# Attention core of a hybrid backbone step: one guard and one transposed copy for both heads, transposes ahead of the values of an older item

## What is computed

```python
def attend_block(qb, keys, values, masks, sink):
    scale = HEAD_DIM ** -0.5
    ...
        s = jnp.einsum('bqkgd,bskd->bkgqs', qb, kp).astype(jnp.float32) * scale
        if mk is not None:
            s = jnp.where(mk, s, NEG_INF)
    ...
    m = sink_f
    for s in scores:
        m = jnp.maximum(m, jnp.max(s, axis=-1))
    denom = jnp.exp(sink_f - m)
    ...
        p = jnp.exp(s - m[..., None])
        denom = denom + jnp.sum(p, axis=-1)
        out = out + jnp.einsum('bkgqs,bskd->bqkgd', p.astype(vp.dtype), vp)
    out = out / jnp.moveaxis(denom, -1, 1)[..., None]
```

## Time and profile before

| | us |
|---|---|
| median of three runs | 2660.65 (2658.5 to 2661.7) |
| profiled execution | 2665.53 |
| its span in the trace | 2663.7 |
| TensorE busy | 2573.9 (97%) |
| TensorE weight loads busy | 2383.5 (89%) |
| VectorE busy | 1984.8 (75%) |
| ScalarE busy | 1299.1 (49%) |
| GpSimd busy | 115.5 (4%) |
| attention core of layer 0 | about 142.8 to 283.9 of the span |
| attention core of layer 3 | about 2013.6 to 2131.6 of the span |

### The profile page before, as it was taken

The page is one execution under the profiler, slowest core; times in us unless marked ns, Lnnn a source line. Parts: engine busy times, 40 slices in busy tenths (PEclk is TensorE's granted clock), DMA queues, the critical chain, the costliest instruction groups (busy, mean ns, idle before and its releaser), DMA issues.

```text
span 2663.7 us, 43103 instructions
## 1 busy us (share of the span) xinstructions
PE 2573.9 (97%) x15856; PEld 2383.5 (89%) x15856; DVE 1984.8 (75%) x3736; ACT 1299.1 (49%) x2291; POOL 115.5 (4%) x146
## 2 busy tenths in 40 slices
PE   6989999999998999999989999999998999999999
PEld 4966899999998999999879999999997699999998
DVE  3777488888896888888855888888868946754772
ACT  3467365425524663355244662454347936633551
POOL 2000100000012000000101000000100010000000
PEclk9999899999998999999989999999999999999999
DMA  7224122433341334434302335334320012222222
GB/s 292 64 95 148 58 101 104 163 138 118 108 168 48 103 110 160 154 105 146 124 21 72 116 111 184 111 110 153 118 71 29 2 56 72 78 87 64 76 83 78
DMA packets 72274, 279.64 MB, mean 105 GB/s; under 512 B 7888, under 2 KB 11344, under 8 KB 68560
## 3 DMA queue, kind: packets, MB, share of 16 engines
q1 hardware_dynamic: 72144, 277.93, 30.5%
HBM read 274.75 MB, written 3.15 MB: 104 GB/s over the span
## 4 chain that ended last, share of the span: by engine, by line
PE 89%; DVE 7%; issue 2%; ACT 1%; DMA 1%; POOL 0%; SPq 0%; DVEq 0%; ACTq 0%
PE ps L575 20%; PE ps L573 16%; PE ps L574 16%; PE ps L576 15%; PE ps L577 11%; PE ps L792 2%; PE ps L777 2%; PE ps L761 1%; PE ps L634 1%; DVE h L1406 1%; PE ps L687 1%; DVE prob L1609 1%; DVE ada_w L1352 1%; PE ps L828 1%; PE ps L569 1%
## 5 line engine op out<-in xcount | busy, mean ns | idle before, releaser
L575 PE MATMUL ps<-h,w_hi 128*128 128x512 f32 x1768 | 700.5, 396 | 0.0
L573 PE MATMUL ps<-h,w_hi 128*128 128x386 f32 x1768 | 604.8, 342 | 8.2 <-DVE h L1406 4.9
L574 PE MATMUL ps<-h,w_hi 128*128 128x386 f32 x1768 | 602.9, 341 | 0.0
L576 PE MATMUL ps<-h,w_lo 128*128 128x386 f32 x1768 | 598.7, 339 | 0.0
L950 ACT ACTIVATE tail<-ps 128x256 f32<-128x256 f32 x281 | 108.3, 386 | 966.0 <-PE ps L577 965.4
L577 PE MATMUL ps<-h,w_lo 128*128 128x256 f32 x1768 | 503.4, 285 | 0.0
L577 PEld LDWEIGHTS ps<-h,w_lo 128*128 128x128 f32 x1768 | 333.7, 189 | 79.6
L1293 DVE TENSOR_TENSOR w_lo<-w_raw,w_hi 128x1024 fp32r<-128x1024 f32 (+1 forms) x288 | 377.4, 1311 | 4.9 <-ACT w_hi L945 1.7
L573 PEld LDWEIGHTS ps<-h,w_hi 128*128 128x128 f32 x1768 | 339.3, 192 | 11.3 <-DVE h L1406 7.2
L574 PEld LDWEIGHTS ps<-h,w_hi 128*128 128x128 f32 x1768 | 335.8, 190 | 0.0
L575 PEld LDWEIGHTS ps<-h,w_hi 128*128 128x128 f32 x1768 | 334.0, 189 | 0.0
(11 more groups left out here) (166 smaller groups left out, 3890.0 us busy)
## 6 DMA issues: line engine op xcount, KB each, us to landing
w_raw<-in_w_in SPq DMA_DIRECT2D x176, 512.0 KB, 3.6
w_raw<-in_w_out SPq DMA_DIRECT2D x64, 704.0 KB, 4.1
ada_w<-in_ada_t SPq DMA_DIRECT2D x42, 1024.0 KB, 6.3
row_w<-in_ada_t SPq DMA_DIRECT2D x60, 512.0 KB, 3.5
ada_w<-in_ada_w SPq DMA_DIRECT2D x18, 1024.0 KB, 5.0
w_raw<-in_w_qkv SPq DMA_DIRECT2D x24, 512.0 KB, 3.5
w_raw<-in_w_o SPq DMA_DIRECT2D x16, 512.0 KB, 3.5
first_w<-in_ada_w SPq DMA_DIRECT2D x6, 1024.0 KB, 14.3
```

What stands on the lines that cost most here:

```text
L573: pe.matmul(main, wh, b[:, 0, 0:MAIN], start=first, stop=False)
L574: pe.matmul(main, wh, b[:, 1, 0:MAIN], start=False, stop=False)
L575: pe.matmul(wide, wh, b[:, :, MAIN:NT], start=first, stop=last, skip_group_check=True)
L576: pe.matmul(main, wl, b[:, 0, 0:MAIN], start=False, stop=last)
```

## The change

Four things are changed, all in the attention core of both layers. `probT` becomes one buffer for both heads of an item. VectorE takes both heads' maxima first and then makes the guard for both at once, in two tensor_tensor over two elements each (times -scale, then minimum with -sink) in place of a fused tensor_scalar per head; `max_made` counts items, and ScalarE waits for it before the first head's exp. ScalarE copies the transposed probabilities of both heads, banks 4 and 5, in one instruction, after the transposes of both; `pt_made` counts items, and TensorE waits for it before the first head's transposes of the next item. And TensorE issues `turn(w-1)` ahead of `values(w-2)`.

```diff
-            probT = [[sb(f"probT{s}{hd}", [P, 512], F32, a) for hd in range(2)] for s in range(2)]
+            probT = [sb(f"probT{s}", [P, 2, 512], F32, a) for s in range(2)]
...
                         if w - w0 >= 2:
-                            pe.wait_ge(max_made, 2 * (w - 1))
+                            pe.wait_ge(max_made, w - 1)
...
                             if w - w0 >= 1:
-                                pe.wait_ge(pt_made, 2 * (w - 1) + hd + 1)
+                                pe.wait_ge(pt_made, w)
...
-                        pe.wait_ge(pt_made, 2 * w + 2)
+                        pe.wait_ge(pt_made, w + 1)
...
                         if w == w0:
                             sum_heads(layer, 9)
+                        if 1 <= w - w0 <= 40:
+                            turn(w - 1)
                         if w - w0 >= 2:
                             values(w - 2)
-                        if 1 <= w - w0 <= 40:
-                            turn(w - 1)
...
                         act.wait_ge(sink_put, w + 1)
+                        act.wait_ge(max_made, w + 1)
                         for hd in range(2):
                             st = stat[:, w % 2, hd, :]
-                            act.wait_ge(max_made, 2 * w + hd + 1)
...
-                        for hd in range(2):
-                            act.wait_ge(t_done, 2 * w + hd + 1)
-                            act.activation(probT[w % 2][hd][:, b0:b1], ps[:, 4 + hd, b0:b1],
-                                           ACT.Copy).then_inc(pt_made, 1)
+                        act.wait_ge(t_done, 2 * w + 2)
+                        act.activation(probT[w % 2][:, :, b0:b1], ps[:, 4:6, b0:b1], ACT.Copy).then_inc(pt_made, 1)
...
-                            head = 8 * ga + 4 * hd + r
-                            if w - w0 < KT and hd == 0:
-                                dve.wait_ge(q_scaled, KT * a + tile + 1)
-                            dve.tensor_scalar(st[:, 1:2], st[:, 0:1], neg_scale[:, tile, nb, hd:hd + 1],
-                                              neg_sink[:, a, head:head + 1],
-                                              ALU.mult, ALU.min).then_inc(max_made, 1)
+                        st, head = stat[:, w % 2, :, :], 8 * ga + r
+                        if w - w0 < KT:
+                            dve.wait_ge(q_scaled, KT * a + tile + 1)
+                        own.link(dve.tensor_tensor(st[:, :, 1], st[:, :, 0], neg_scale[:, tile, nb, :], ALU.mult))
+                        dve.tensor_tensor(st[:, :, 1], st[:, :, 1], neg_sink[:, a, head:head + 5:4],
+                                          ALU.min).then_inc(max_made, 1)
```

## The result

The changed kernel takes 2671.67 us (median of six runs, 2671.21 to 2678.39) against 2661.19 us for the kernel before in the runs beside it: a ratio of 1.0039, 95% interval 1.0028 to 1.0050, or 10.5 us more. The forecast was 2672.4 us. One execution was profiled, with a span of 2670.2 us.

The account below looks back on a forecast made before the run. TensorE, busy 97% of the span, was taken as the bound; a new loop of waits was to add 11.3 us in layer 3 and 0.4 in layer 0, 2660.65 + 11.7 = 2672.4 us, range 2664 to 2679.

Parts of the forecast that it names:

- The loop: Attention core, once per item: transposes, values, out_hi, copy, next transposes; 3.49 us with four blocks, 2.83 with three, 1.54 with one.
- The copy's length: ScalarE's merged copy from PSUM: estimated at 1.02 us for 1024 elements, 0.81 for 768 and 0.38 for 256.
- The guard: VectorE gets 0.1 to 0.2 us per item back from the new guard; nothing booked, since VectorE doesn't set the pace.
- The sum: Both attention cores: layer 3 +11.3 us and layer 0 +0.4, added to the median 2660.65 as +11.7, giving 2672.4.
- Order and merged copy together close it: Four-block items, layer 3: the loop takes 3.49 us; with two copies 3.07, under TensorE's 3.12.
- (a): Rival: waits for out_lo were the cost, the new loop doesn't bind; layer 0 -5.4 us, layer 3 stays, 2655.2; chance 0.05.
- (b): Rival: layer 3 loses 11.3 us as forecast, layer 0 gains its full 5.4, 2666.6 us; chance 0.12.
- (c): Rival: TensorE's idle time in layer 3 drops the clock to 1.2 GHz, 40 us more, 2712 us; chance 0.04.

## Why the prediction was right, point by point

*The loop.* Right in each link: out_hi 0.12 us behind the values, the copy 0.17 behind it (0.16 foreseen), the next transposes 0.14 behind the copy; 3.47 us in all for 3.49. Three-block items come every 2.82 us (2028.32 to 2031.14 and on) for 2.83. In layer 0, where the conditioning product hides it in every other item, the pairs take what was worked out, 6.30 and 7.60 us:

```profile
162.89 0.66 PE L792 MATMUL ps<-probT,v_tok 128*64 128x128 f32 x8
...
169.19 0.66 PE L792 MATMUL ps<-probT,v_tok 128*64 128x128 f32 x8
...
190.45 0.88 PE L792 MATMUL ps<-probT,v_tok 128*64 128x128 f32 x12
...
198.05 0.88 PE L792 MATMUL ps<-probT,v_tok 128*64 128x128 f32 x12
```

*The copy's length.* 1.02 and 0.81 us were taken from the slope between two widths in the earlier trace rows. ScalarE's group of the changed kernel (busy us, mean ns):

```profile
L1111 ACT ACTIVATE probT<-ps 128x1024 f32<-128x1024 f32 x32 | 32.6, 1019 | 0.1
```

*The guard.* 0.16 us per tensor_tensor as the row of another line had it (0.162 and 0.164 in the groups of the changed kernel), and nothing to be seen in the total, as booked. With the loop open it is worth some microseconds, in the items of three blocks and of one.

*The sum.* Layer 3's core +12.1 for +11.3, layer 0's +0.1 for +0.4, together 12.2 for 11.7. The medians are 10.5 apart, with an interval from 7.5 to 13.3. Inside layer 3 four terms were off and offset each other, and that the total came within a microsecond is luck to that extent. The first three-block group came to +3.0 for +1.7: its first step took 3.49 us, half of it at the lower clock, and its last two 3.04 and 3.26, with work of the four-block items already in them. And 1.3 us more pass from the first scores to the first values (17.1 for 15.8), since these now stand behind the second item's transposes; I had booked nothing for the start of the pipeline. The four-block items came to +5.9 for +6.6, mostly since the last two steps of the group are shorter ones (3.25 and 3.04). The one-block items came to -0.5 for +0.8: most of them ran at the full clock, and I had taken the middle. Three of their steps took 1.73 us for the loop's 1.54, with TensorE waiting for VectorE's probabilities and not for the copy. Layer 0's +0.1 is a sum of the same kind: +0.8 for +1.0 in the four-block items, -1.4 for -0.6 in those of three, and +0.9 at the start for nothing.

*The sentence that failed.* "Order and merged copy together close it." True of the loop through out_hi, as the order alone leaves items at 3.12 us; but I read from it that the order was a condition of the cost, and it isn't. In the old order the merged copy closes a second, shorter way (transposes 0.17 us into the scores, copy 1.03, 0.14 to the values, beside scores of 1.07), and costs 11 us by itself. The rows were there: in the earlier trace rows the two copies end only 0.26 us ahead of the values that need them, so a copy that begins some 0.4 us later, behind the second head's transposes, had to be late. The forecast isn't touched by this, since its sum takes only the loop of the new order.

*The rivals.* (a) fell: the waits for out_lo did go (1.5 us for 7.0), but the loop took their place in layer 0. The 22.3 us named in its favour overstate what was to be had, as the idle time of the weight loads is counted in them; its own price of 5.4 us was worked out from two steps of the timeline. With the loop open, in the kernel with the copy ahead of out_hi, they turn into the gain that (a) promised and more, -8.0 us in layer 0. (b) fell by the pairs of 7.60 us. (c) fell: TensorE idle for 1.7 us of 20, and even for 3.0 of 20 with the spare operation, kept a granted clock of 1.00.

*Fewer or shorter instructions.* By the Trainium skill, ScalarE: Activation LUTs, section What ACT_TABLE_LOAD costs, the merged copy was to take 1.04 us and save 0.09, an estimate from its figures; it takes 1.02 and saves 0.06 (two copies were 1.08), and that is of no use here. The Trainium skill, Perfetto Trace Analysis, section Optimizing Scalar/DVE Operations, says that where ScalarE isn't saturated but makes other engines wait, breaking up its instructions may let work finish sooner. This case bears it out: breaking the copy up again brought 11.2 us. Moving the copy ahead in ScalarE's queue brought 17, with the copy left whole.

## What to carry to other kernels

Before merging two instructions into one, look at what begins with the first half and what waits for the end: the saving is the fixed part of one instruction, the price is the overlap of half of it, and the merging is free only where the wait for the end is covered by other work. When two engines' queues are written by hand and one is reordered, walk once round the other: an instruction that became late (out_hi here) holds up whatever stands behind it, and the cure may be to swap those two instead of undoing the change. A loop of waits shows in the profile as no engine full, each idle once per item behind the next; its period is the sum of its links, and a spare operation put into one link tells in one run whether it is on it.

## What the runs showed of the hardware

A copy that reads two PSUM banks in one instruction runs at the rate of one that reads a single bank: 1.019 us for 2 x 512 elements, on the line through 0.488 for 384 and 0.595 for 512. A spare ScalarE operation of 0.30 us, put between out_hi and the copy, delays the copy by only 0.20 us. With TensorE idle for up to 3.0 us of 20, in pieces of about half a microsecond, the granted clock stayed at 1.00; at the start of layer 3's core it was at 0.50, and it came back 0.2 us behind the first values in one kernel and 3.1 behind in another, worth 1.3 us. And two executions of unedited code, some 1730 us of it between the attention cores, differed by 3.2 us, with the same instructions; effects of a few microseconds are to be read in the stage, not from two spans.
